# Tile 0 of a conditioned decoder step: routing in one step, taps on VectorE, a seventh unit buffer, and the cached rows' copy in 4 KB pieces

## The chip, the cores and the metric

The kernel runs on one core of a Trainium2 chip. The metric is the time of one execution on the device in microseconds (us); several executions are timed and the median counts. A profiled execution gives, beside its own time, the time of every instruction and of every DMA packet.

## The reference, cut to what matters

One layer of a decoder is applied to 512 prompt rows and to 8 x 4 sample rows, all float32, model width 1024.

```
h   = rms_norm(x) * (1 + scale1) + shift1
z   = h @ w_in                      # q, six k/v column groups, gates, conv input (glu)
o_attn = compressed, selected and windowed attention, gated
u   = glu_a * sigmoid(glu_b);  y[t] = sum_k conv_w[k] * u[t + k] + conv_b    # 31 taps, 512 channels
x  += gate1 * concat(rms_norm(o_attn), silu(layer_norm(y)) * scale) @ w_out
h2  = rms_norm(x) * (1 + scale2) + shift2
q   = (h2 @ q_w).reshape(8 heads, 2, 128);  s = q . sub_keys      # 128 scores for each of 2 halves
s1, i1 = top_k(s[0], 16);  s2, i2 = top_k(s[1], 16)
top_s, pos = top_k(all 256 sums of s1 and s2, 16);  expert = i1 * 128 + i2 at pos
x  += gate2 * sum over 8 heads x 16 experts of softmax(top_s) * gelu(h2 . u[expert]) * v[expert]
new_win_sample = the cached window rows moved up by 4, then 4 new rows; other caches likewise
```

For each of 8 samples `new_win_sample` takes over 508 cached rows of 1 KB each (2 x 2 x 64 floats) unchanged. That is a copy from HBM to HBM of 8 x 520 KB, and no arithmetic depends on it.

## The kernel before, in words

The rows are worked in five tiles, four of 128 prompt rows and one of 32 sample rows. Each of tiles 0 to 3 has 8 x 16 = 128 experts per row, and the sample tile 32 more steps, 544 steps in all. One step gathers from HBM, for every partition, the 8 KB of one expert (u and v), 1 MB for the tile, into one of ten ring rows (`expert_rows`, GpSimd's indirect DMA at L2777). VectorE multiplies u with h2 and sums (L2724), ScalarE makes gelu, weight and a diagonal, and TensorE adds the weighted v into PSUM (L1460).

Everything else of a tile ("side work") is written as stages: `x`, `glu`, `z`, `cmp`, `att`, `conv`, `mix` (the product with w_out, L1189), `query0` and `query1` (the product with q_w, L1205, and the scores, L1292 and L1264), and `topk0` and `topk1` (the routing of four heads each). `make_plan` lays the stages into windows of slots; lanes of one item run side by side, and every engine runs its part of each slot in that one order. Window 0 and the one behind it hold all of tile 0 up to `topk0`; no expert step is consumed before that is through, since there are no experts yet. From then on slots are dealt out between the steps.

**Weights** come in units of 1 MB (128 partitions x 8 KB) into few homes. `weight_units` lists the units in the order of use: `ada` (adaLN), `in`, `w1`, `wo`, `pq` (q_w). `homes_of` gives each the home that was used longest ago: three slots of `weight_units`, and early in the program three more, ring row 4 (`EARLY_ROW`), `h_rows` and `gate_or_shift_and_scale`. SyncE (SP) issues all plain loads and stores from one queue in one order (`sp_program`). For each unit it first does what `aside(key)` says, then waits until TensorE has used the home's unit before, then issues.

**Tile 0 is special.** `topk0` runs in two steps of two heads (`routed`), so that GpSimd can begin gathering after the first. The keys for the scores are loaded into `mod_a` and `mod_b` (L2910, L2913), outside the unit order. Of the 31 taps over four groups of 128 channels, GpSimd does the first two groups (L2754, L2756) and VectorE the other two (L2198, L2201). The cached rows' copy (L2914, 4 MB) is issued before the load of unit `pq` 3, with outermost dimension 8 (one for each sample):

```
if key == ("pq", 0, 3):
    sp.wait_ge(e.s_h2, 1)
    sp.dma_start(e.mod_b, io["keys_unit"][:, D:]).then_inc(e.s_k0[1], 16)
    sp.dma_start(io["new_win_sample"][0, :, 0:WIN - DT].rearrange("b w a g d -> b w (a g d)"),
                 io["cache_win_kv"][0, :, DT:].rearrange("b w a g d -> b w (a g d)")).then_inc(e.s_store, 16)
```

## Time and profile before

| | us |
|---|---|
| median of 3 executions | 2018.53 (2012.03 to 2022.49) |
| the profiled execution | 2007.81, its span 2005.9 |
| TensorE busy | 1472.7 (73%) |
| VectorE busy | 1259.0 (63%) |
| GpSimd busy | 839.2 (42%) |
| ScalarE busy | 760.7 (38%) |
| moved by DMA | 756.73 MB, mean 377 GB/s |

The profile has a page with the busy share of each engine and of the 16 DMA engines in 40 slices of the span. Other views give windows of any length with the DMA engines' mean busy share and rate, the instructions of an engine in order of time with the idle time before each and what ended it, DMA issues with their sizes, and groups of instructions by line.

### The profile page before, as it was taken

Reading aid. Unit: us, or ns where it says so; the run is one execution under the profiler, and the core shown is the slowest. Engines: PE = TensorE matmul, PEld = TensorE weight load, DVE = VectorE, ACT = ScalarE, POOL = GpSimd, SP = SyncE. Lnnn points to the kernel's source line nnn. Section 1 sums busy time; section 2 is a strip of 40 time slices with the busy share of each in tenths; the row PEclk is TensorE's granted clock in tenths of the full one; section 3 lists DMA queues with packets and bytes.
Section 4 is the critical chain, followed back from the end, with each engine's and each line's share of the span. In section 5 each row is a group of like instructions: output and inputs, shape, how many; then the busy total and the mean of one; then the engine's idle time right before and its main releaser. Section 6 shows DMA issues by size and latency. Waiting matters only on the chain.

```text
span 2005.9 us, 27852 instructions
## 1 busy us (share of the span) xinstructions
PE 1472.7 (73%) x9567; PEld 829.9 (41%) x9567; DVE 1259.0 (63%) x3345; ACT 760.7 (38%) x2179; POOL 839.2 (42%) x738
## 2 busy tenths in 40 slices
PE   7775677878679897958667879775979685866532
PEld 4644544445445443535313446443545241423100
DVE  1564585965888689935996645883456554343754
ACT  1431244853265466733236642231222233242322
POOL 0520032433334354523333432772764767432532
PEclk9878788888889898878868989797999878786866
DMA  9778889999999899999999999898999999999996
GB/s 394 253 265 307 330 357 420 402 383 388 420 397 403 345 417 407 396 412 382 419 421 379 420 405 392 319 416 313 353 407 381 394 406 339 399 412 379 371 411 274
DMA packets 132287, 756.73 MB, mean 377 GB/s; under 512 B 17134, under 2 KB 36494, under 8 KB 46050
## 3 DMA queue, kind: packets, MB, share of 16 engines
q0 software_dynamic: 82432, 578.86, 71.6%
q1 hardware_dynamic: 49715, 176.10, 22.8%
q8 instruction: 77, 1.26, 0.3%
q14 instruction: 63, 0.52, 0.1%
HBM read 750.19 MB, written 9.29 MB: 379 GB/s over the span
## 4 chain that ended last, share of the span: by engine, by line
PE 33%; DMA 20%; DVE 16%; issue 7%; POOL 5%; ACT 5%; SPq 0%; POOLq 0%; ACTq 0%; DVEq 0%
PE bank L1460 12%; DMA expert_rows<-in_expert_uv,expert_index 11%; DVE expert_rows L2724 6%; PE bank L1333 4%; PE bank L1205 3%; POOL expert_rows L2777 3%; PE bank L857 3%; PE bank L1189 3%; POOL weight_units L2781 2%; DMA gate_or_shift_and_scale<-mod_dram 2%; PE bank L794 2%; DMA weight_units<-in_w_out_units 1%; DMA weight_units<-in_peer_q_units 1%; DVE gate_or_shift_and_scale L2201 1%; DMA out_y_prompt<-x_rows 1%
## 5 line engine op out<-in xcount | busy, mean ns | idle before, releaser
L2777 POOL DMA_INDIRECT expert_rows<-in_expert_uv,expert_index x544 | 648.5, 1192 | 1027.4 <-PE bank L1460 806.0
L2724 DVE CUSTOM_DVE_ANT_0 expert_rows<-expert_rows,h_rows 128x1024 f32<-128x1024 f32 x544 | 659.7, 1221 | 357.8 <-DMA expert_rows<-in_expert_uv,expert_index 349.5
L1460 PE MATMUL bank<-expert_rows,weight_diagonals 64*64 64x512 f32 x4096 | 589.2, 701 | 127.5 <-ACT weight_diagonals L2042 105.1
L2022 ACT ACTIVATE group_gelu<-group_dots 128x2 f32<-128x2 f32 x272 | 55.1, 203 | 763.8 <-DVE group_dots L2724 759.8
L1460 PEld LDWEIGHTS bank<-expert_rows,weight_diagonals 64*64 64x64 f32 x4096 | 149.4, 150 | 412.4 <-issue 221.7
L2042 ACT ACTIVATE weight_diagonals<-consts_sb,group_weights 128x64 f32<-128x64 f32 (+1 forms) x544 | 158.1, 338 | 17.0 <-ACT group_weights L2032 0.4
L1205 PE MATMUL bank<-stage_room,weight_units 128*128 128x128 f32 x1024 | 130.9, 288 | 34.8 <-DMA weight_units<-in_peer_q_units 33.2
L1205 PEld LDWEIGHTS bank<-stage_room,weight_units 128*128 128x128 f32 x1024 | 124.2, 201 | 58.0 <-DMA weight_units<-in_peer_q_units 37.3
L2032 ACT ACTIVATE group_weights<-group_gelu,expert_gate 128x1 f32<-128x1 f32 x544 | 130.5, 287 | 9.5
L2201 DVE SCALAR_TENSOR_TENSOR conv_out<-stage_room,small_weights,conv_out 128x128 f32<-128x128 f32 (+1 forms) x420 | 125.7, 347 | 0.1
L2022 ACT ACT_TABLE_LOAD x74 | 94.9, 1283 | 1.3
L1189 PE MATMUL bank<-weight_units,stage_room 128*128 128x256 f32 (+1 forms) x304 | 75.1, 406 | 21.7 <-issue 10.3
L1189 PEld LDWEIGHTS bank<-weight_units,stage_room 128*128 128x128 f32 (+1 forms) x304 | 54.6, 184 | 48.4 <-issue 21.6
L1463 PE MATMUL bank<-expert_rows,weight_diagonals 128*32 128x512 f32 x128 | 28.9, 1053 | 55.3 <-ACT weight_diagonals L2042 42.1
L1333 PE MATMUL bank<-weight_units,prompt_bias 128*128 128x256 f32 x256 | 64.7, 403 | 0.0
L1333 PE MATMUL bank<-weight_units,stage_room 128*128 128x256 f32 x256 | 61.7, 393 | 0.0
L857 PE MATMUL bank<-weight_units,stage_room 128*128 128x256 f32 (+1 forms) x240 | 58.5, 396 | 3.1 <-issue 3.1
L2527 DVE MAX8 stage_room<-stage_room 128x8 f32<-128x128 f32 (+1 forms) x102 | 27.5, 325 | 50.1 <-ACT stage_room L1909 25.3
L1333 PEld LDWEIGHTS bank<-weight_units,prompt_bias 128*128 128x128 f32 x256 | 49.0, 199 | 20.0 <-issue 13.8
L1333 PEld LDWEIGHTS bank<-weight_units,stage_room 128*128 128x128 f32 x256 | 48.1, 194 | 16.4 <-issue 10.5
L2476 DVE TENSOR_TENSOR stage_room<-bank,gate_or_shift_and_scale 128x256 f32<-128x256 f32 (+1 forms) x20 | 8.4, 422 | 67.5 <-PE bank L1189 67.5
L857 PEld LDWEIGHTS bank<-weight_units,stage_room 128*128 128x128 f32 (+1 forms) x240 | 39.2, 170 | 25.4 <-issue 14.1
(387 smaller groups left out, 2003.6 us busy)
## 6 DMA issues: line engine op xcount, KB each, us to landing
weight_units<-in_peer_q_units SPq DMA_DIRECT2D x40, 1024.0 KB
weight_units<-in_w_in_units SPq DMA_DIRECT2D x22, 1024.0 KB
weight_units<-in_w_out_units SPq DMA_DIRECT2D x19, 1024.0 KB
weight_units<-in_w_ada_units SPq DMA_DIRECT2D x14, 1024.0 KB
weight_units<-in_w_units SPq DMA_DIRECT2D x11, 1024.0 KB
expert_rows<-in_expert_uv,expert_index POOLq DMA_INDIRECT x544, 12.1
gate_or_shift_and_scale<-mod_dram SPq DMA_DIRECT2D x11, 512.0 KB
expert_rows<-in_w_ada_units SPq DMA_DIRECT2D x5, 1024.0 KB, 6.7
```

Source lines behind the costliest of these rows:

```text
L794: last = mm(out[:, 0:TOKENS], w[:, k, a * P:(a + 1) * P], e.hT[i][:, k * TOKENS:(k + 1) * TOKENS], start=(k == 0), stop=(k == KD - 1))
L857: last = mm(out[0:r, c * 256:(c + 1) * 256], hT(t, k), w[:, k], start=(k == 0), stop=(k == KD - 1))
L1189: last = mm(out[0:r, 0:256], e.catT[:, k, 0:r], w[:, k], start=(k == 0), stop=(k == KD - 1))
L1205: last = mm(out[:, c:c + r], w[:, k, a * P:(a + 1) * P], e.h2T[:, k, 0:r], start=(k == 0), stop=(k == KD - 1))
L1333: last = mm(dst, w1[:, one, s, hh * P:(hh + 1) * P], w[:, :, :, s], start=False, stop=(one == 1 and s == 7))
L1460: last = mm(e.bank[2 * a + c][o * HD:(o + 1) * HD, :], e.diag[ps, m % (NG * GR)], e.ring[ps, m % RING, cs], start=first, stop=final)
L2022: do(e.act_v[:, p], e.dots[:, p], ACT.Gelu_apprx_tanh).then_inc(e.s_gelu, 1)
L2032: do(e.wv[:, p, j:j + 1], e.act_v[:, p, j:j + 1], ACT.Copy, scale=e.gsm[:, i % 2, o + j:o + j + 1]).then_inc(e.s_w, 1)
L2042: do(e.diag[:, p * GR + j, 0:unit.shape[1]], unit, ACT.Copy, scale=e.wv[:, p, j:j + 1]).then_inc(e.s_d, 1)
L2201: ins = vec.scalar_tensor_tensor(out, src, w[:, ct, k:k + 1], out, ALU.mult, ALU.add)
L2724: vec.tensor_tensor_reduce(out=row, in0=row, in1=e.h2[:, i % 2], scale=1.0, scalar=0.0, op0=ALU.mult, op1=ALU.add, accum_out=e.dots[:, q % ...
L2777: pool.indirect_dma_start(e.ring[:, n % RING], None, e.io["expert_uv"], bass.IndirectOffsetOnAxis(ap=e.eidx[:, i % 2, j:j + 1], axis=0)).t ...
```

## The change

Five edits, all in the part of tile 0 ahead of the first expert step.

1. `topk0` of tile 0 is one step of four heads, as in the other tiles. The plan runs `query0`, then `query1` beside `topk0`. TensorE computes all four `pq` units of a half before its scores.
2. The keys come as units of the common order (`keys`, 0, half) into the three slots, and no more into `mod_a` and `mod_b`.
3. VectorE does all 124 taps, by pairs of channel groups, beginning when two groups of conv input are there. GpSimd does none.
4. Ring row 5, which GpSimd's taps used, becomes one more home for early units (seven in all).
5. The cached rows' copy is issued at unit `wo` 0, ahead of the four `wo` loads, in pieces of four rows (4 KB), with the piece's number (127) as outermost dimension and the sample (8) inside it. Loading gate2's rows moves from `pq` 7 to `in` 6 of tile 1.

```diff
-EARLY_HOMES = 6
-EARLY_ROW = 4
+EARLY_ROWS = (4, 5)
+EARLY_HOMES = SLOTS + len(EARLY_ROWS) + 2
...
-        "query0": lambda i: [("pq", i, u) for u in range(4)] + ([("keys", i, 0)] if 0 < i < PT else []),
+        "query0": lambda i: [("pq", i, u) for u in range(4)] + ([("keys", i, 0)] if i < PT else []),
...
-        homes = list(range(SLOTS)) + [3] * (j < row_until) + [4] * (j < h2_until) + [5] * (j < mods_until)
+        homes = list(range(SLOTS)) + [3, 4] * (j < row_until) + [5] * (j < h2_until) + [6] * (j < mods_until)
...
+    def conv_first(slots, w):
+        n = 0
+        for pair in ((0, 1), (2, 3)):
+            e.early.freed(dve, ("glu", 0, pair[1], 0))
+            for k in range(CK):
+                for ct in pair:
+                    out, src = e.convo[:, ct], e.cu[:, ct, k:k + P]
+                    if k == 0:
+                        ins = vec.tensor_scalar(out, src, w[:, ct, 0:1], w[:, ct, CK:CK + 1], ALU.mult, ALU.add)
+                    else:
+                        dve.wait_ge(e.s_tap, n - 1)
+                        ins = vec.scalar_tensor_tensor(out, src, w[:, ct, k:k + 1], out, ALU.mult, ALU.add)
+                    ins.then_inc(e.s_tap, 1)
...
-        if key == ("pq", 0, 2):
-            sp.wait_ge(e.s_x1, 1)
-            sp.dma_start(e.mod_a, io["keys_unit"][:, 0:D]).then_inc(e.s_k0[0], 16)
-        if key == ("pq", 0, 3):
-            sp.wait_ge(e.s_h2, 1)
-            sp.dma_start(e.mod_b, io["keys_unit"][:, D:]).then_inc(e.s_k0[1], 16)
-            sp.dma_start(io["new_win_sample"][0, :, 0:WIN - DT].rearrange("b w a g d -> b w (a g d)"),
-                         io["cache_win_kv"][0, :, DT:].rearrange("b w a g d -> b w (a g d)")).then_inc(e.s_store, 16)
+        if key == ("wo", 0, 0):
+            sp.dma_start(io["new_win_sample"][0, :, 0:WIN - DT].rearrange("b (u w) a g d -> u b (w a g d)", w=DT),
+                         io["cache_win_kv"][0, :, DT:].rearrange("b (u w) a g d -> u b (w a g d)", w=DT)
+                         ).then_inc(e.s_store, 16)
             sp.dma_start(io["new_conv_sample"][0, :, 0:CK - 1 - DT, :], io["state_conv"][0, :, DT:, :]
                          ).then_inc(e.s_store, 16)
```

**SP's order.** Before, the copy stands behind the `wo`, `ada` and first `pq` loads. The last number of a row is the shape that the instruction carries.

```order
L2800 DMA weight_units<-in_w_ada_units 128x2048 x3
L2808 DMA weight_units<-in_peer_q_units 128x2048 x2
L2910 DMA gate_or_shift_and_scale<-in_keys_unit 128x1024
L2808 DMA weight_units<-in_peer_q_units 128x2048
L2913 DMA gate_or_shift_and_scale<-in_keys_unit 128x1024
L2914 DMA out_new_win_sample<-in_cache_win_kv 8x8x16256
L2916 DMA out_new_conv_sample<-in_state_conv 8x13312
L2808 DMA weight_units<-in_peer_q_units 128x2048 x4
```

Now it stands behind the last `ada` unit of the second group (u = 19), and all four `wo` loads, the rows of shift and scale, the last `ada` loads and all `pq` loads are behind it.

```order
L2745 DMA h_rows<-in_w_ada_units 128x2048
L2854 DMA out_new_win_sample<-in_cache_win_kv 127x8x1024
L2857 DMA out_new_conv_sample<-in_state_conv 8x13312
L2774 DMA gate_or_shift_and_scale<-mod_dram 128x1024
L2751 DMA weight_units<-in_w_out_units 128x2048 x3
L2784 DMA mod_dram<-expert_rows 9x1024
L2751 DMA expert_rows<-in_w_out_units 128x2048
L2784 DMA mod_dram<-expert_rows 9x1024
L2774 DMA expert_rows<-mod_dram 128x1024
L2774 DMA gate_or_shift_and_scale<-mod_dram 128x1024
L2745 DMA expert_rows<-in_w_ada_units 128x2048
```

The copy moved past the fourteen loads between, and its outermost count went from 8 to 127.

**TensorE from h2 to the first expert step.** L1205 and L1199 are the product with q_w (16 matmuls a unit, which the trace shows as 32), L1292, L1264 and L1255 the scores. Before:

```order
L1276 MATMUL bank<-consts_sb,h_rows 128x128 x8
L1205 MATMUL bank<-stage_room,weight_units 128x128 x32
L1292 MATMUL bank<-gate_or_shift_and_scale,stage_room 128x128 x4
L1205 MATMUL bank<-stage_room,weight_units 128x128 x32
L1292 MATMUL bank<-gate_or_shift_and_scale,stage_room 128x128 x4
L1205 MATMUL bank<-stage_room,weight_units 128x128 x64
L1264 MATMUL bank<-gate_or_shift_and_scale,stage_room 128x128 x8
```

Now:

```order
L1267 MATMUL bank<-consts_sb,h_rows 128x128 x8
L1199 MATMUL bank<-stage_room,weight_units 128x128 x64
L1255 MATMUL bank<-weight_units,stage_room 128x128 x8
L1199 MATMUL bank<-stage_room,weight_units 128x128 x64
L1255 MATMUL bank<-weight_units,stage_room 128x128 x8
```

The first scores moved from behind two units to behind four, and the keys are read from the unit slots.

## Rows read from the trace of the kernel before

**Rows 1.** The page: DMA share in tenths and rate, in 40 slices of the span.

```profile
DMA  9778889999999899999999999898999999999996
GB/s 394 253 265 307 330 357 420 402 383 388 420 397 403 345 417 407 396 412 382 419 421 379 420 405 392 319 416 313 353 407 381 394 406 339 399 412 379 371 411 274
```

**Rows 2.** Windows: length, busy us of PE, PEld, DVE, ACT, POOL, clock, DMA share, GB/s.

```profile
186.00:192.00 6.00, 0.00 (x0) 0.00 (x0) 5.69 (x17) 0.23 (x1) 0.00 (x0) 0.50 0.43 184
190.00:194.00 4.00, 0.00 (x0) 0.00 (x0) 3.73 (x10) 0.00 (x0) 0.00 (x0) 0.50 0.52 223
...
200.00:205.00 5.00, 5.00 (x26) 5.00 (x25) 0.00 (x0) 0.00 (x0) 3.78 (x5) 0.50 1.01 421
240.00:245.00 5.00, 1.38 (x7) 1.39 (x8) 3.56 (x16) 2.78 (x5) 0.00 (x0) 0.76 0.33 139
245.00:250.00 5.00, 2.86 (x13) 2.46 (x12) 4.90 (x21) 4.85 (x13) 0.00 (x0) 0.50 0.00 0
```

**Rows 3.** TensorE in order of time: start, length, what, idle before and its releaser.

```profile
141.34 6.50 PE L1189 MATMUL bank<-h_rows,stage_room 128*128 128x256 f32 x16 [4.24 <-DVE stage_room L2468]
...
168.01 7.41 PE L1205 MATMUL bank<-stage_room,weight_units 128*128 128x128 f32 x64 [0.73 <-ACT stage_room L1861]
176.14 1.13 PE L1292 MATMUL bank<-gate_or_shift_and_scale,stage_room 128*128 128x128 f32 x8 [0.72 <-issue]
177.11 3.74 PE L1205 MATMUL bank<-stage_room,weight_units 128*128 128x128 f32 x32
199.01 6.69 PE L1205 MATMUL bank<-stage_room,weight_units 128*128 128x128 f32 x32 [18.16 <-DMA weight_units<-in_peer_q_units]
...
229.98 6.57 PE L1205 MATMUL bank<-stage_room,weight_units 128*128 128x128 f32 x32 [10.95 <-DMA weight_units<-in_peer_q_units]
```

**Rows 4.** SP's queue in order of time.

```profile
122.70 0.33 SPq L2800 DMA_DIRECT2D expert_rows<-in_w_ada_units  x1
...
166.19 0.88 SPq L2914 DMA_DIRECT2D out_new_win_sample<-in_cache_win_kv  x1
...
171.88 34.18 SPq L2808 DMA_DIRECT2D weight_units<-in_peer_q_units  x4
```

**Rows 5.** DMA issues of 0 to 300 us: count, KB each, median us to landing.

```profile
out_new_win_sample<-in_cache_win_kv SPq DMA_DIRECT2D x1, 4064.0 KB
...
small_weights<-in_small SPq DMA_DIRECT2D x1, 487.0 KB, 4.3
out_new_conv_sample<-in_state_conv SPq DMA_DIRECT2D x1, 416.0 KB
expert_rows<-in_expert_uv,expert_index POOLq DMA_INDIRECT x24, 14.3
```

**Rows 6.** VectorE's taps: five beside GpSimd's taps, what stands behind them, five alone.

```profile
89.77 3.75 DVE L2201 SCALAR_TENSOR_TENSOR conv_out<-stage_room,small_weights,conv_out 128x128 f32<-128x128 f32 x5
...
94.95 0.15 DVE L2302 TENSOR_TENSOR hidden_bias<-bank,small_weights 128x4 f32<-128x4 f32 x1
...
121.83 1.38 DVE L2201 SCALAR_TENSOR_TENSOR conv_out<-stage_room,small_weights,conv_out 128x128 f32<-128x128 f32 x5
```

**Rows 7.** VectorE: a routing step of two heads, a grid operation of four, step 0's dot.

```profile
177.92 0.87 DVE L2527 MAX8 stage_room<-stage_room 128x8 f32<-128x128 f32 x4 [11.22 <-ACT stage_room L1909]
...
188.79 0.69 DVE L2564 TENSOR_TENSOR stage_room<-stage_room,consts_sb 128x512 f32<-128x512 f32 x1
...
193.37 0.18 DVE L2572 CAST expert_index<-stage_room 128x32 int32<-128x32 f32 x1
...
239.97 1.23 DVE L2724 CUSTOM_DVE_ANT_0 expert_rows<-expert_rows,h_rows 128x1024 f32<-128x1024 f32 x1
...
282.33 1.23 DVE L2564 TENSOR_TENSOR stage_room<-stage_room,consts_sb 128x1024 f32<-128x1024 f32 x1
```

**Rows 8.** GpSimd: the first gather and the eleventh.

```profile
194.49 1.11 POOL L2777 DMA_INDIRECT expert_rows<-in_expert_uv,expert_index  x1 [77.88 <-DVE expert_index L2572]
...
...
257.05 1.90 POOL L2777 DMA_INDIRECT expert_rows<-in_expert_uv,expert_index  x1 [50.26 <-PE bank L1460]
```

More of the change, by code:

```diff
@@ L341, in memory @@
     x_odd = e.sb("odd_x_rows", [P, D])
-    e.homes = [e.unit[:, j] for j in range(SLOTS)] + [e.ring[:, EARLY_ROW], e.h2[:].rearrange("p a n -> p (a n)"), team]
+    e.homes = [e.unit[:, j] for j in range(SLOTS)]
+    e.homes += [e.ring[:, a] for a in EARLY_ROWS] + [e.h2[:].rearrange("p a n -> p (a n)"), team]
     e.xr = [(x_even, x_odd)[i % 2] for i in range(TILES)]
@@ L1282, in query0 @@
             yield from sample_queries(0)
-            return
-        if i == 0:
-            for q in range(2):
-                yield from queries(i, range(2 * q, 2 * q + 2))
-                if q == 0:
-                    keys = key_half(i, 0)
-                prod.freed(pe, ("pq", i, q))
-                out = prod.open(pe, ("scores", i, q))
-                for a in range(4):
-                    last = mm(out[:, a * P:(a + 1) * P], e.q2T[:, 4 * q + a, 0:P], keys[:, 4 * q + a], start=True, stop=True)
-                last.then_inc(prod.ready, 1)
-                yield
             return
@@ L1899, in query_half @@
             return
-        if i == 0 and half == 0:
-            for q in range(2):
-                for _ in range(8):
-                    yield
-                out = prod.wait(act, ("pq", i, q))
-                nc.scalar.copy(e.q2T[:, 4 * q:4 * q + 4].rearrange("p a n -> p (a n)"), out[:]
-                               ).then_inc(prod.free(("pq", i, q)), 1)
-                yield
-                out = prod.wait(act, ("scores", i, q))
-                nc.scalar.copy(e.scores[0][:, 4 * q:4 * q + 4].rearrange("p a n -> p (a n)"), out[:]
-                               ).then_inc(prod.free(("scores", i, q)), 1)
-            return
         for q in range(2 * half, 2 * half + 2):
@@ L1927, in topk @@
     def topk(i, part):
-        if i == 0 and part == 0:
-            for a in range(2):
-                for _ in range(7 if a == 0 else 10):
-                    yield
-                act.wait_ge(e.s_sx if a else e.s_sx0, 1)
-                g = e.gsm[:, 0, 2 * a * TK:2 * (a + 1) * TK]
-                do(g, g, ACT.Exp).then_inc(e.s_gx if a else e.s_gx0, 1)
-            return
         n = 4 if i < PT else 2
@@ L2178, in conv @@
         if i == 0:
-            e.early.freed(dve, ("glu", i, 3, 0))
-        elif i < LATE:
+            yield from conv_first(slots, w)
+            return
+        if i < LATE:
             prod.freed(dve, ("glu", i, 3))
@@ L2188, in conv @@
             link(vec.tensor_copy(e.cs[:, :, :, CK - 1:], e.us[:].rearrange("p c (b t) -> p c b t", b=NB)))
-        cts = range(2, 4) if i == 0 else range(4)
-        total = len(cts) * CK
-        for n in range(total):
-            k, ct = n // len(cts), cts[n % len(cts)]
+        for n in range(4 * CK):
+            k, ct = n // 4, n % 4
             if i < PT:
@@ L2745, in pool_program @@
 def pool_program(e, pool):
-    each = e.nc.gpsimd
-    link = Chain(pool, e.s_pch)
-    w = e.col("conv").rearrange("p (c k) -> p c k", c=4)[:, 0:2]
-    cu, convo = e.cu[:, 0:2], e.convo[:, 0:2]
-    part = e.ring[:, 5, 0:2 * P].rearrange("p (c n) -> p c n", c=2)
-    e.early.freed(pool, ("glu", 0, 1, 0))
-    for k in range(CK):
-        link(each.tensor_tensor(part if k else convo, cu[:, :, k:k + P], span(w[:, :, k], 2, P), ALU.mult))
-        add = part if k else span(w[:, :, CK], 2, P)
-        ins = each.tensor_tensor(convo, convo, add, ALU.add)
-        if k + 1 < CK:
-            link(ins)
-    ins.then_inc(e.s_pc, 1)
-    pool.wait_ge(e.s_pc, 1)
     for m in range(3):
         pool.wait_ge(e.s_md[m], 16)
-    pool.wait_ge(*e.given[max(j for j, home in enumerate(e.home) if home == SLOTS)])
+    for a in range(SLOTS, SLOTS + len(EARLY_ROWS)):
+        pool.wait_ge(*e.given[max(j for j, home in enumerate(e.home) if home == a)])
     due = pool_pages(e)
```

86 lines of the change are left out of this document (30 added, 56 removed).

## The prediction

> **What bounds the kernel now.** I read the slices first, to see what is scarce over the whole span. The DMA engines are busy for nine tenths or more of most slices, and the best rate, about 421 GB/s, appears in many of them [rows 1]. The second view is the windows, for the stretches where that is not so. All of them lie in tile 0, ahead of and just behind the first expert step: 0.43 to 0.52 of the DMA engines while the cached rows are copied, nothing at all from 245 to 250 us [rows 2]. The third view is TensorE in order of time. From 141.3 us, the first `wo` product, the path runs through TensorE: `wo`, the last `ada`, h2, the queries, scores, routing, first dot at 239.97 [rows 3, 7]. It holds two large waits for weights, 18.16 us for unit `pq` 3 and 10.95 us for `pq` 7 [rows 3]. Behind the first dot the plan deals out the same slots to the same steps in both kernels, so what the change does to the total is by how much it moves that first dot, and what DMA work is still owed then.
>
> **The copy (edit 5) is the term that decides.** Before, it is issued at 166.19, and `pq` 3, first of four loads issued from 171.88 on, is used only at 199.01 [rows 3, 4]. Near its end, with next to nothing beside it, the DMA share is 0.52 and 0.43 at 223 and 184 GB/s [rows 2]. That is 7 to 8 of 16 engines, each at its full pace: 421 / 16 = 26.3 GB/s in the full window, 223 / 8 = 27.9 here. The instruction carries 8x8x16256, outermost count 8. So the copy is cut along its outermost dimension, one share for each of 8 engines, and 4064 KB [rows 5], 4.16 MB, take 0.52 MB / 26.3 GB/s = 20 us on each. A load issued behind it must pass through all 16 engines, waits in the same queues, and is as late as its share on the busiest.
>
> Now the outermost count is 127, with 8 inside. If shares must be equal, 127 (a prime) can be dealt to one engine or to 127, and there are 16: the whole copy goes through one. It then takes 4.16 MB / 26.3 GB/s = 158 us. Bounds: 149 us at 27.9 GB/s for an engine, 181 us at 184 / 8 = 23. The pieces shrink from 65 KB to 4 KB; no row has a piece of 4 KB from HBM to HBM, and units of 8 KB rows move at the full 421 GB/s [rows 2], so I add nothing for it and let the 181 us stand for it. I take equal shares: the rows show a hard cut by the outermost count, which left half of the engines without work although each sample's 520 KB was itself in eight rows of 65 KB. They cannot exclude shares of 8, 8, ... 7, since 8 is dealt out evenly either way; that is the first rival.
>
> The Trainium skill, page "DMA: Bandwidth & Descriptors", section "Queues, rings and completion order" with the one on why a DMA adds 16 to its semaphore, states just this rule: for a DMA from SP the slowest dimension picks the largest number of engines up to 16 that divides it, and 127 gives 1. The trace agrees for a count of 8; no row here shows a count that 16 engines cannot share evenly.
>
> When is it issued? Before, the last `ada` load of that group (u = 19) leaves at 122.70 [rows 4]; it waited for TensorE to use the unit that held its home. With seven homes it waits for a unit one earlier, and the compress branch ahead of it moves up too (next part). I take 112 us, between 107 and 122.7, and add 2.5 us for that 1 MB unit (1.05 MB / 421 GB/s) which is ahead in the queues. The copy ends at 112 + 2.5 + 158 = 272.5. On the same engine stand behind it the conv history (416 KB on 8 engines [rows 5], 52 KB each, 2.0 us), gate1's rows (512 KB on 16, 1.2 us) and `wo` 0 (2.5 us), and about 1 us until TensorE sees it: 279.2. TensorE began `wo` 0 at 141.34 [rows 3]. **The stall is 137.9 us**; bounds 107 + 149 + 8 = 264 gives +123, 122.7 + 2.5 + 181 + 7 = 313 gives +172.
>
> What else is queued: SP waits, ahead of the rows of shift2, for a 36 KB store of `mod_dram` that also sits behind the copy, so the last four `ada` loads leave only then. They need 10 us of DMA, and TensorE spends more than that on the four `wo` units (6.50 us on the first alone [rows 3]), so I add 1 us. From `wo` 0 to the first query product nothing else changes: 168.01 - 141.34 = 26.7 us.
>
> **Taps on VectorE (edit 3).** Beside GpSimd's taps five cost 3.75 us, alone 1.38 [rows 6], 0.28 each. Before, about half of VectorE's 62 taps ran at the slow pace and half at the fast, 31 x 0.75 + 31 x 0.28 = 32 us; now 124 x 0.28 = 34 us, begun some 12 us earlier. What stands behind them moves up: `hidden_bias` at 94.95 [rows 6] now comes behind 49 fast taps, 13.6 us, with the attention's own operations between them, near 92. Down the chain (compressed keys, their attention) I get 4 us at `wo` 0, bounds 0 and 7. In this branch it is worth nothing in itself, since `wo` 0 waits for the copy 140 us longer; it only brings the copy's issue forward. Were that cover gone, it would count in full. The seventh home (edit 4) likewise: one 1 MB load earlier, no wait of its own removed.
>
> **Queries, keys and routing (edits 1 and 2).** From the first query product on, in us behind it. Before: four units and the wait up to the second scores, then the first dot at 239.97 - 168.01 = 72.0 [rows 3, 7]. Now: four `pq` units back to back, 7.41 + 2 x 3.74 = 14.9. Can the loads follow? A unit needs 2.5 us of DMA and about 2 us to land (487 KB landed in 4.3 us [rows 5]); three slots give it 7 us, so yes. Scores and their copy to VectorE: in the rows 175.42 to 177.92, 2.5. Routing four heads: two heads took 177.92 to 193.55, 15.6; twice that is 31.2, less 7 x (2 x 0.69 - 1.23 = 0.15) = 1.0 for the grid operations done once [rows 7], less 1.4 for a dozen small ones: 28.8. GpSimd starts 0.9 later (193.55 to 194.49 [rows 8]), and the first 1 MB lands behind 5.5 us, bounds 4.3 and 14.3 [rows 5]. Sum 14.9 + 2.5 + 28.8 + 0.9 + 5.5 = 52.6, against 72.0: **a gain of 19.4 us**, bounds 11 and 21. The second half (`query1`) ends near 35 and is off the path.
>
> What was gathered early was worth nothing: ten gathers from 194.49 fill the ring, the eleventh waits until 257.05 [rows 8], and meanwhile they took 10 MB x 1 / 421 GB/s = 25 us of DMA in front of `pq` 7, hence its 10.95 us. But they are owed now. At the first dot the new kernel is about 10 MB behind, some 25 us; before, the DMA engines idled there: 0.33 and 0.00 of them from 240 to 250 [rows 2], and the ring was full until 257.05 [rows 8], in all some 15 us. Steps follow each other there at about 3.6 us and use 1 MB each, so gathers keep ahead; units of tile 1 come late by what is left. I charge 3 us, less 1.4 us since x of tile 1 is normed before the dot and not behind it: +1.6, bounds 0 and 9.
>
> **Sum.** 137.9 + 1 - 19.4 + 1.6 = **+121 us**. Against the profiled execution: 2007.8 + 121 = 2129. That execution was 10.7 us under the median of the three, and medians are compared, so I forecast 2018.5 + 121 = **2139 us**. Lowest: 123 - 21 - 6 (spread of the three) = +96, 2114; I take 2110. Highest: 172 + 1 - 11 + 9 = +171, 2189; I take 2187.
>
> **Rivals.**
>
> *A, the copy is spread.* If 127 is dealt as 8, 8, ... 7, or along the dimension of 8, it takes 10 to 20 us from 112 on, when the DMA engines were idle or half idle, and the `wo` loads land 5 us or more before 141. For it: the rows bear uneven shares as well, and each other edit removes a wait that is plain in the trace. Against: the eight engines follow the outermost count. Then edits 3 and 4 count: -4 - 19.4 + 1.6 = -22: 1997 us, faster. 0.15.
>
> *B, spread, but the debt eats the gain.* The ten gathers and tile 1's units meet in one burst: first landing 14.3 in place of 5.5, debt 9 in place of 3, no gain from the taps: -19.4 + 8.8 + 7.6 = -3: 2016 us, no change. For it: the slices behind 260 us are at 400 GB/s and more [rows 1], so there is little room to catch up. It decides if the first landing takes over 10 us. 0.03.
>
> *C, one engine, and its small pieces are dear.* If a 4 KB piece costs more than its bytes, say 0.25 us in place of 0.156, 1016 pieces take 254 us and the time is 2235. Against: both sides of the transfer are plain rows. 0.02.
>
> **How the numbers follow.** One engine at the priced rate 0.80, A 0.15, B 0.03, C 0.02; the copy is either on one engine or spread, and the half-empty windows of rows 2 speak for a strict deal by the outermost count. The likeliest gives 2139. Its range 2110 to 2187 holds nearly all of its 0.80, so it is given alone. A measurement of this kernel can tell about 0.5%, 10 us, from no change: faster 0.15, same 0.03, slower 0.82.
>
> **What would show it.** In the profile of the changed kernel: a stretch of 120 us or more before the first `wo` product with TensorE idle and a DMA share near 1/16, about 26 GB/s; its wait put down to the `wo` load. Then `pq` units with no wait on DMA, one routing of four heads some 29 us long, the first gather about 47 us behind the first query product, the first dot near 53. Taps at 0.28 us with `hidden_bias` near 92 us. From the first dot on the same lengths as before. The forecast is wrong if the DMA share stays at a half or more behind the copy's issue and the `wo` products start near 137: then it is rival A.

## The result, and the profile after

| | before | after |
|---|---|---|
| median of 4 executions, us | 2015.28 | 2135.14 |
| the profiled execution, and its span | 2007.81, 2005.9 | 2132.21, 2130.4 |
| mean rate of DMA over the span, GB/s | 377 | 355 |

The ratio is 1.0592, with a 95% interval of 1.0527 to 1.0657: the changed kernel is 120 us slower. One of its four executions, 2178.09 us at a mean granted clock of 0.735 where the others have 0.81 to 0.82, is left out of the ratio. The forecast was 2139 with a range of 2110 to 2187.

The page of the changed kernel answers to [rows 1]. The third to fifth of its 40 slices of 53 us hold the loss:

```profile
DMA  9720077999999998999999999989899999999996
GB/s 399 254 97 26 36 280 286 420 421 404 347 377 417 385 418 344 418 396 397 414 419 421 383 420 408 396 332 412 312 372 402 388 396 378 355 408 374 401 413 279
```

In windows (columns as in [rows 2]) the copy shows as one sixteenth of the DMA engines at 26 to 27 GB/s, for as long as it runs. From 262.5 us on the loads behind it are issued and pass on the other engines, up to the full rate, while the copy still runs on its own. A second lull at 275 to 285 us is that one engine's share of these loads:

```profile
120.00:140.00 20.00, 7.87 (x67) 5.27 (x66) 10.74 (x34) 8.64 (x20) 0.00 (x0) 0.72 0.07 27
140.00:160.00 20.00, 0.00 (x0) 0.00 (x0) 0.00 (x0) 0.00 (x0) 0.00 (x0) 0.50 0.06 26
...
270.00:275.00 5.00, 0.00 (x0) 0.00 (x0) 0.00 (x0) 0.00 (x0) 0.00 (x0) 0.50 1.01 427
275.00:280.00 5.00, 0.00 (x0) 0.00 (x0) 0.00 (x0) 0.00 (x0) 0.00 (x0) 0.50 0.53 223
280.00:285.00 5.00, 2.85 (x7) 2.35 (x8) 0.00 (x0) 0.00 (x0) 0.00 (x0) 0.50 0.06 26
```

SP's queue, which answers to [rows 4]. L2854 issues the copy. L2857, the conv history behind it, is 149.64 us in the issuing itself: SP can hand over no further DMA until most of the copy has gone.

```profile
111.43 0.49 SPq L2745 DMA_DIRECT2D h_rows<-in_w_ada_units  x1
111.96 0.84 SPq L2854 DMA_DIRECT2D out_new_win_sample<-in_cache_win_kv  x1
112.86 149.64 SPq L2857 DMA_DIRECT2D out_new_conv_sample<-in_state_conv  x1
262.61 0.63 SPq L2774 DMA_DIRECT2D gate_or_shift_and_scale<-mod_dram  x1
263.29 4.14 SPq L2751 DMA_DIRECT2D weight_units<-in_w_out_units  x3
```

TensorE, which answers to [rows 3]. L1183 is the product with w_out, at 282.15 in place of 141.34, and L1199 is the product with q_w, in which no unit waits for its load any more:

```profile
132.93 1.97 PE L1174 MATMUL bank<-consts_sb,stage_room 128*128 128x128 f32 x8 [6.30 <-DVE stage_room L2436]
282.15 12.37 PE L1183 MATMUL bank<-weight_units,stage_room 128*128 128x256 f32 x48 [147.25 <-issue]
...
308.32 14.56 PE L1199 MATMUL bank<-stage_room,weight_units 128*128 128x128 f32 x128 [0.72 <-ACT stage_room L1840]
323.60 2.02 PE L1255 MATMUL bank<-weight_units,stage_room 128*128 128x128 f32 x16 [0.72 <-issue]
```

The wait of 147.25 us is put down to "issue", so to nothing that the profile shows, and not to the `wo` load. That the load ended it is read from the queue and the packets: its issue begins at 263.29; seven of the conv history's eight pieces run from 263.3 on, and the eighth, which shares the copy's engine, only from 276.03 to 278.00; the next loads, `wo` 0 among them, come behind it in the same queue.

VectorE, which answers to [rows 6] and [rows 7] (taps, hidden_bias, routing of four heads from its first MAX8 to its indices, first dot), and GpSimd, which answers to [rows 8] (first and eleventh gather):

```profile
78.99 3.76 DVE L2140 SCALAR_TENSOR_TENSOR conv_out<-stage_room,small_weights,conv_out 128x128 f32<-128x128 f32 x14
...
95.74 0.15 DVE L2275 TENSOR_TENSOR hidden_bias<-bank,small_weights 128x4 f32<-128x4 f32 x1
```

```profile
325.39 0.88 DVE L2490 MAX8 stage_room<-stage_room 128x8 f32<-128x128 f32 x4 [18.36 <-ACT stage_room L1890]
...
354.14 0.20 DVE L2535 CAST expert_index<-stage_room 128x64 int32<-128x64 f32 x1
...
361.19 1.23 DVE L2687 CUSTOM_DVE_ANT_0 expert_rows<-expert_rows,h_rows 128x1024 f32<-128x1024 f32 x1 [5.47 <-DMA expert_rows<-in_expert_uv,expert_index]
```

```profile
355.27 1.07 POOL L2722 DMA_INDIRECT expert_rows<-in_expert_uv,expert_index  x1 [354.81 <-DVE expert_index L2535]
...
376.08 0.94 POOL L2722 DMA_INDIRECT expert_rows<-in_expert_uv,expert_index  x1 [7.39 <-PE bank L1439]
```

The first dot is at 361.19 in place of 239.97, 121.2 us later; the span is 124.5 us longer. All but 3.3 us of the loss is there before the first expert step.

### The profile page after: what moved, and what is told of

Its sections match the earlier page's. It is cut to its first block, busy times and chain, and to the rows that moved or that the text cites. A ratio compares the mean times of both kernels' runs of the same rounds, so it can differ in the third digit from the quotient of the medians.

```text
span 2130.4 us, 27830 instructions
## 1 busy us (share of the span) xinstructions
PE 1476.8 (69%) x9567; PEld 830.8 (39%) x9567; DVE 1257.3 (59%) x3390; ACT 760.4 (36%) x2178; POOL 787.3 (37%) x676
## 3 DMA queue, kind: packets, MB, share of 16 engines
q1 hardware_dynamic: 50660, 176.10, 21.5%
## 4 chain that ended last, share of the span: by engine, by line
PE 33%; DMA 15%; DVE 15%; issue 7%; ACT 6%; POOL 6%; SPq 0%; POOLq 0%; ACTq 0%; DVEq 0%
PE bank L1439 12%; DMA expert_rows<-in_expert_uv,expert_index 10%; DVE expert_rows L2687 5%; PE bank L1312 4%; POOL weight_units L2726 3%; POOL expert_rows L2722 3%; PE bank L1183 3%; PE bank L1199 3%; PE bank L853 2%; DMA weight_units<-in_peer_q_units 2%; PE bank L790 2%; PE bank L1119 1%; DMA gate_or_shift_and_scale<-mod_dram 1%; DVE gate_or_shift_and_scale L2174 1%; ACT stage_room L1772 1%
## 5 line engine op out<-in xcount | busy, mean ns | idle before, releaser
L1439 PE MATMUL bank<-expert_rows,weight_diagonals 64*64 64x512 f32 x4096 | 592.0, 704 | 132.1 <-ACT weight_diagonals L1997 109.7
L1183 PE MATMUL bank<-weight_units,stage_room 128*128 128x256 f32 (+1 forms) x304 | 79.0, 422 | 159.7 <-issue 150.6
L1183 PEld LDWEIGHTS bank<-weight_units,stage_room 128*128 128x128 f32 (+1 forms) x304 | 57.8, 195 | 186.5 <-issue 161.3
L1199 PEld LDWEIGHTS bank<-stage_room,weight_units 128*128 128x128 f32 x1024 | 118.8, 194 | 28.3 <-issue 19.5
L1199 PE MATMUL bank<-stage_room,weight_units 128*128 128x128 f32 x1024 | 124.8, 281 | 4.9 <-DMA weight_units<-in_peer_q_units 3.3
L2174 DVE SCALAR_TENSOR_TENSOR conv_out<-stage_room,small_weights,conv_out 128x128 f32<-128x128 f32 (+1 forms) x360 | 95.6, 312 | 0.0
L1119 PE MATMUL bank<-prompt_keys_values,queries_turned 64*128 64x256 f32 (+2 forms) x96 | 48.5, 606 | 2.8 <-ACT stage_room L1787 2.8
```

The source lines that it names most:

```text
L1119: last = mm(out[:, c:c + m], q, k[lo:lo + HD, 0:m], start=True, stop=True)
L1183: last = mm(out[0:r, 0:256], e.catT[:, k, 0:r], w[:, k], start=(k == 0), stop=(k == KD - 1))
L1199: last = mm(out[:, c:c + r], w[:, k, a * P:(a + 1) * P], e.h2T[:, k, 0:r], start=(k == 0), stop=(k == KD - 1))
L1439: last = mm(e.bank[2 * a + c][o * HD:(o + 1) * HD, :], e.diag[ps, m % (NG * GR)], e.ring[ps, m % RING, cs], start=first, stop=final)
L2174: ins = vec.scalar_tensor_tensor(out, src, w[:, ct, k:k + 1], out, ALU.mult, ALU.add)
```

## Experiments

Ratios are to the kernel before, measured on the same chip as each group of runs: 2022.3 us for the first four, 2024.8 for the next four (GpSimd's taps, six homes, two steps, 254), 2012.4 for the last four. Times of different groups compare by these ratios. "First query product" is the first product with q_w, "first dot" the dot of step 0.

### 1. What makes the copy slow: count, piece or place

Four kernels, each the changed one with nothing but the copy's form altered; both access patterns are rearranged alike.

**Outermost count 8 again**, at the new place:

```diff
-  ...rearrange("b (u w) a g d -> u b (w a g d)", w=DT)
+  ...rearrange("b w a g d -> b w (a g d)")
```

> The changed kernel with one thing put back: the cached rows' copy has the outermost count 8 again (8x8x16256 in place of 127x8x1024), at its new place ahead of `wo` 0. Theory (the outermost count sets how many DMA engines share the copy): it ends some 20 us behind its issue at 112, `wo` 0 begins near 139 in place of 282, so 143 us come back: 2135 - 143 = 1992 us, 1985 to 2003. Rival (the new place costs: any copy of 4 MB ahead of `wo` 0 holds it up): 20 to 40 us of the stall stay, 2012 to 2032.

Measured: 2001.35 us, ratio 0.9896 (0.9862 to 0.9931). 134 us less than the changed kernel, so nearly all of the 143 came back. `wo` 0 begins at 144.38 and not at 139, and it waited 9.16 us:

```profile
144.38 13.23 PE L1183 MATMUL bank<-weight_units,stage_room 128*128 128x256 f32 x48 [9.16 <-issue]
```

Its window from 135 to 140 us has half of the engines free, as [rows 2] had:

```profile
135.00:140.00 5.00, 0.22 (x2) 0.00 (x0) 0.69 (x1) 3.34 (x8) 0.00 (x0) 0.50 0.33 140
```

So most of the stall was the count. What is left of the wait is the copy's on 8 engines at this place: 5.2 us, 9.16 against the 3.92 of the next kernel.

**Outermost counts 112 and 15**, pieces of 4 KB kept:

```diff
+            for first, last, w in ((0, 448, 4), (448, 508, 4)):
+                sp.dma_start(io["new_win_sample"][0, :, first:last].rearrange("b (u w) a g d -> u b (w a g d)", w=w),
+                             io["cache_win_kv"][0, :, DT + first:DT + last].rearrange("b (u w) a g d -> u b (w a g d)", w=w)
+                             ).then_inc(e.s_store, 16)
```

> The changed kernel with its 4 KB pieces, at its new place, in two DMAs of outermost counts 112 and 15 in place of one of 127 (448 and 60 rows of each sample). Theory (outermost count): 112 is shared by 16 engines and 15 by 15, all pieces at 0.155 us make 1016 x 0.155 / 16 = 10 us, `wo` 0 near 139, 1992 us, 1985 to 2003. Rival (4 KB pieces from HBM to HBM are what is slow, or pile up in SP's queue): the stretch of TensorE idle stays over 50 us and the time over 2040.

Measured: 2000.76 us, ratio 0.9908 (0.9869 to 0.9947). `wo` 0 and the first dot:

```profile
137.63 12.44 PE L1183 MATMUL bank<-weight_units,stage_room 128*128 128x256 f32 x48 [3.92 <-DVE stage_room L2441]
```

```profile
217.79 1.22 DVE L2687 CUSTOM_DVE_ANT_0 expert_rows<-expert_rows,h_rows 128x1024 f32<-128x1024 f32 x1 [5.41 <-DMA expert_rows<-in_expert_uv,expert_index]
```

The same 1016 pieces of 4 KB at the same place, and the stall is gone: `wo` 0 waits for VectorE and no more for a load. Neither the size of the pieces nor the place was the cause.

**Outermost count 126**, one piece a sample less in the large DMA (the edit is the loop above over `((0, 504, 4), (504, 508, 1))`):

> The changed kernel with one 4 KB piece a sample taken out of the large DMA: outermost count 126 (504 rows of each sample) and a second DMA of the last 4 rows with outermost count 4. Theory (the engines are the largest number up to 16 that divides the outermost count): 126 goes to 14 engines, 1008 pieces x 0.155 / 14 = 11 us, 1992 us, 1985 to 2003. Rival (any count over 16 that isn't a multiple of 16 goes to one engine, or to few): one engine, 2135 us; 126 mod 16 = 14 alone tells nothing apart from it, one busy engine in 14 would.

Measured: 1998.48 us, ratio 0.987 (0.9801 to 0.9938).

```profile
138.01 12.37 PE L1183 MATMUL bank<-weight_units,stage_room 128*128 128x256 f32 x48 [3.92 <-DVE stage_room L2441]
```

126 is fast and 127 is not. That falls in with the rule that the engines must divide the outermost count (126 = 14 x 9), and refutes one engine for every count that isn't a multiple of 16. The trace's DMA packets show the number itself: from 121 to 128 us mostly 14 pieces of 4 KB are under way at a time, in the kernel with 112 and 15 mostly 16.

**Outermost count 254**, pieces of 2 rows (`w=2`):

> The changed kernel with the copy cut in pieces of 2 rows, 2 KB, outermost count 254 in place of 127 (254x8x512). Theory (largest number up to 16 that divides the count): 254 gives 2 engines, 2032 pieces in all, 1016 on each; if a 2 KB piece takes half of 0.155 us the copy lasts 79 us and the rate is 53 GB/s, `wo` 0 begins near 205 and the time is near 2058; if a 2 KB piece takes as long as one of 4 KB, it lasts 158 us at 26 GB/s, 2135 us. Rival (any count that 16 doesn't divide goes to one engine): one engine, 158 us at least, 2135 us or more, at 26 GB/s too; the number of pieces under way at a time tells these apart.

Measured: 2058.73 us, one execution; forecast 2058. The rate while it runs, `wo` 0, and SP's issue of the next DMA:

```profile
140.00:160.00 20.00, 0.00 (x0) 0.00 (x0) 0.00 (x0) 0.00 (x0) 0.00 (x0) 0.50 0.13 51
```

```profile
204.83 12.77 PE L1183 MATMUL bank<-weight_units,stage_room 128*128 128x256 f32 x48 [71.46 <-issue]
```

```profile
111.56 78.09 SPq L2858 DMA_DIRECT2D out_new_conv_sample<-in_state_conv  x1
```

Share 0.13, two sixteenths: two engines, the largest number up to 16 that divides 254 = 2 x 127. The trace has 125 packets of 2 KB in 5 us, so 0.080 us each on an engine, against 32 of 4 KB in 5 us, 0.155 us each, with 127: bytes, not pieces, set the time. Four counts, 8, 126, 254 and 127, with 8, 14, 2 and 1 pieces under way at a time, are told apart as the largest number up to 16 that divides the count says.

### 2. The same form at the old place

```diff
 if key == ("pq", 0, 3):
-    ...rearrange("b w a g d -> b w (a g d)")
+    ...rearrange("b (u w) a g d -> u b (w a g d)", w=DT)
```

> The kernel before with one thing changed: the cached rows' copy, at its old place behind `pq` 3, as 127x8x1024. Theory (one engine for 158 us): issued at 166 the copy ends near 327, SP and the loads of `pq` 3 and on are held, `pq` 3 begins near 331 in place of 199, +132 us, less up to 11 us for the wait ahead of `pq` 7 that has gone by then: 2136 to 2150 us. Rival (the harm of the change lies in its new place): under 2060.

Measured: 2173.04 us, ratio 1.073 (1.0654 to 1.0805). The form alone costs more here than in the changed kernel, and more than I expected. Unit `pq` 3, and two windows of the copy:

```profile
366.54 5.60 PE L1205 MATMUL bank<-stage_room,weight_units 128*128 128x128 f32 x32 [180.87 <-DMA weight_units<-in_peer_q_units]
```

```profile
200.00:250.00 50.00, 0.00 (x0) 0.00 (x0) 0.00 (x0) 0.00 (x0) 8.85 (x10) 0.50 0.55 223
250.00:300.00 50.00, 0.00 (x0) 0.00 (x0) 0.00 (x0) 0.00 (x0) 0.00 (x0) 0.50 0.06 26
```

From 200 to 250 GpSimd's ten gathers get through while SP's loads do not, and the copy pays: 23 of its pieces pass in 10 us from 210 to 240, against 64 or 65 alone, counted in the trace's DMA packets. Some 35 us at that pace put off (6.4 - 2.3) x 35 = 143 pieces, 143 x 0.155 = 22 us. I had left that out. Of the 35.5 us by which `pq` 3 is later than I gave, this is most; the copy's later issue (170.82, I took 166) is 5 more, and the rest isn't told apart. The ten gathers used the engine by another queue than SP's; that is the next experiment.

### 3. The same copy through another queue

The 127x8x1024 copy is issued by ScalarE, behind its copy of tile 0's compressed keys.

```diff
         nc.scalar.copy(e.kcT[:, 0:hi], out[:, 0:hi]).then_inc(prod.free(("kcT", i)), 1)
+        if i == 0:
+            nc.scalar.dma_start(...same two access patterns...).then_inc(e.s_store, 16)
```

> The changed kernel with the 127x8x1024 copy issued from ScalarE's DMA queue (behind its copy of the compressed keys of tile 0, near 108 us) and not from SP's; all else as changed. Theory (the copy is on one engine, and the loads are held because they stand behind it in the same queue; an engine takes two queues in turn, as the gathers passed the copy in the run of before with 127): a unit's share on that engine takes 8 x (0.309 + 0.155) = 3.7 us in place of 2.5, `wo` 0 begins at 138 to 142, the copy lasts up to 158 x 64/23 = 440 us, and while it does DMA runs at two thirds of its rate: the first dot at 218 to 230, the total 2010 to 2060. Rival (the engine itself is shut while the copy is on it, whichever queue it came by): `wo` 0 near 282, 2135 us.

Measured: 2096.52 us, one execution. The front is as the theory says, `wo` 0 at 137.30, so the engine isn't shut. The tail is dearer than I gave it: the time is 36 us above the top of my range, 2060. The same windows, first of this kernel, then of the one with 112 and 15:

```profile
137.30 12.50 PE L1183 MATMUL bank<-weight_units,stage_room 128*128 128x256 f32 x48 [3.92 <-DVE stage_room L2446]
```

```profile
260.00:360.00 100.00, 57.16 (x326) 29.27 (x326) 52.71 (x131) 31.65 (x81) 19.68 (x19) 0.78 0.79 306
400.00:500.00 100.00, 64.21 (x325) 32.17 (x325) 60.43 (x196) 45.57 (x132) 21.74 (x20) 0.69 0.64 238
```

```profile
260.00:360.00 100.00, 78.33 (x486) 41.29 (x487) 75.14 (x207) 51.12 (x145) 35.39 (x30) 0.79 1.01 421
400.00:500.00 100.00, 81.13 (x580) 54.65 (x580) 57.60 (x159) 35.01 (x102) 33.04 (x29) 0.91 0.98 394
```

The copy's packets run from 109.7 to 590 us, 480 in place of 158. As long as they do, the whole core gets 306 and 238 GB/s in place of 421 and 394. My reading is that every 1 MB load or gather is as late as its share on that one engine; the trace does not name the engine of a packet, so this is argued. That the copy is the cause is seen from when the loss arises: the first dot is at 228.99, 11.2 us behind the kernel with 112 and 15, the hundredth step, at 585 us, is 120 us behind, and from there to the end, with the copy gone, the distance grows no more (105 to 117 us). So two things stalled the changed kernel: one engine for the whole copy, and the order of SP's queue, which made all of it come before the `wo` loads. Another queue takes the second away and spreads the first over 480 us.

### 4. What the other edits are worth

Here the copy is in the 112 and 15 form, so that it hides nothing, in all kernels but the first. That one is the kernel before once more, for its trace:

> The kernel before once more, for its trace on the same chip. Theory (the trace of before that the rows come from was of an execution in which TensorE's products of the first `in` unit ran at the full granted clock, while every later trace has them at half until 43 us): here they are at half too, `wo` 0 begins near 146 in place of 141.3, the first dot near 245 in place of 240, and the time is nearer 2022 than 2008. Rival (the slow stretch comes with the changed kernel's order): `wo` 0 at 141.3.

Measured: 2008.91 us, one execution. TensorE's first `in` unit, `wo` 0, unit `pq` 3, and VectorE's first dot:

```profile
38.55 5.87 PE L948 MATMUL bank<-weight_units,expert_rows 128*128 128x256 f32 x16 [2.02 <-ACT expert_rows L1547]
...
146.58 6.46 PE L1189 MATMUL bank<-h_rows,stage_room 128*128 128x256 f32 x16 [4.16 <-DVE stage_room L2468]
...
204.39 6.58 PE L1205 MATMUL bank<-stage_room,weight_units 128*128 128x128 f32 x32 [18.36 <-DMA weight_units<-in_peer_q_units]
```

```profile
245.60 1.22 DVE L2724 CUSTOM_DVE_ANT_0 expert_rows<-expert_rows,h_rows 128x1024 f32<-128x1024 f32 x1
```

Half of the theory held: the products of the first `in` unit are slow here too, `wo` 0 is at 146.58 and the first dot at 245.60. The other half did not: the time is 2008.91, no nearer to 2022. The trace that the rows ahead of the prediction come from is the odd one, with

```profile
36.17 3.72 PE L948 MATMUL bank<-weight_units,expert_rows 128*128 128x256 f32 x16 [2.02 <-ACT expert_rows L1547]
```

In all thirteen other traces, of the changed kernel and of every experiment, the first products are 0.427 us apart until 41 to 43 us and 0.216 then. That is the granted clock. In nine of these traces the windows show it, as in this one of the kernel before with its copy spread (the last experiment below): 0.50, which is 1.2 GHz, up to 43.1 us, then 1.00, which is 2.4 GHz.

```profile
38.00:41.00 3.00, 3.00 (x8) 2.37 (x9) 0.00 (x0) 0.00 (x0) 0.00 (x0) 0.50 0.98 415
44.00:47.00 3.00, 3.00 (x16) 2.64 (x15) 0.00 (x0) 0.00 (x0) 0.00 (x0) 1.00 1.01 418
```

In the other four, among them the trace of the changed kernel and this second one of before, the trace holds no record of the clock before 42.6 to 43.4 us, and a window without a record reads 1.00, whatever the clock was; from the first record on the pace is the fast one. In the odd trace that first record is at 30.95 us. So its clock rose some 11 us earlier, and why it did stays open. What follows for the comparison: differences at the first dot are better taken against 245.6 than against 240.

**GpSimd's taps and six homes again** (edits 3 and 4 undone, the code of before in `conv`, `pool_program` and `homes_of`):

> The kernel of the 112 and 15 copy, with edits 3 and 4 undone: GpSimd's half of the taps and six homes, as before; routing in one step and keys as units stay. Theory (the taps bring 4 us at `wo` 0, the routing 19 to 20 at the first dot): `wo` 0 begins at 141 in place of 137.6, the first dot at 221.5 in place of 217.8, total 2005 against 2001. Rival (the taps bring all the gain, the routing is hidden): first dot near 236.

Measured: 2011.22 us, ratio 0.9924 (0.9891 to 0.9958). SP's copy, `wo` 0, first dot:

```profile
125.77 1.77 SPq L2853 DMA_DIRECT2D out_new_win_sample<-in_cache_win_kv  x2
```

```profile
151.66 5.33 PE L1185 MATMUL bank<-h_rows,stage_room 128*128 128x256 f32 x16 [11.09 <-issue]
```

```profile
231.44 1.23 DVE L2671 CUSTOM_DVE_ANT_0 expert_rows<-expert_rows,h_rows 128x1024 f32<-128x1024 f32 x1 [5.54 <-DMA expert_rows<-in_expert_uv,expert_index]
```

Both were wrong: with routing in one step the taps are worth 13.6 us at the first dot, not 4. They let SP issue the copy at 110.7 in place of 125.8, and only so does it end ahead of the `wo` loads' due time. With it in front at 125.8, `wo` 0 waits 11.09 us.

**Six homes alone**, taps on VectorE:

```diff
-EARLY_ROWS = (4, 5)
+EARLY_ROWS = (4,)
```

> The kernel of the 112 and 15 copy, with the seventh home (edit 4) undone, all else kept. Theory (the seventh home removes no wait of its own): `wo` 0 within 1.5 us of 137.6, first dot within 1.5 us of 217.8, total 2001. Rival (it is what sets the earlier loads of tile 0 free): `wo` 0 3 us or more later. The slow TensorE stretch of the traces with seven homes (products of the first `in` unit at half the granted clock up to 43 us) belongs to the loads' order if it goes away here, to the run if it stays.

Measured: 1997.7 us, ratio 0.9875 (0.9824 to 0.9925), `wo` 0 at 137.04, first dot at 217.93, 0.1 us from 217.79. The seventh home is worth nothing here. The slow first products stay, so they do not come with seven homes.

**Routing in two steps** (edits 1 and 2 undone; taps, homes and the copy at `wo` 0 kept):

> The kernel before, with edits 3 and 4 (all taps on VectorE, seven homes) and the cached rows' copy in two DMAs of 112 and 15 ahead of `wo` 0; queries, keys and routing in two steps stay as before. Theory (the 18.16 us wait for `pq` 3 was the copy's and the keys', the 10.95 us wait for `pq` 7 the first ten gathers'): the first of the two waits shrinks to under 5 us since no copy is queued there, the second stays, and the first dot comes near 240 - 4 - 14 = 222, total near 2005. Then the gain of 19 us that was put down to the routing belongs mostly to the copy's place. Rival (routing in one step itself brings it): first dot at 232 or later, total near 2012.

Measured: 1998.49 us, ratio 0.9892 (0.9836 to 0.9948).

```profile
215.27 1.23 DVE L2740 CUSTOM_DVE_ANT_0 expert_rows<-expert_rows,h_rows 128x1024 f32<-128x1024 f32 x1
```

The first dot is 2.5 us earlier than with one step, and from the first query product (166.19) on it takes 49.1 us, against 52.8. Both waits for `pq` units are gone, the one that I expected to stay too. What is left are some 5 us of small gaps between the products of the last `pq` units, from 200 to 207 us, put down to "issue". Routing in one step brings nothing once the copy is out of the way.

**The kernel before with the copy alone moved ahead of `wo` 0**:

> The kernel before with the copy and the conv history alone moved ahead of `wo` 0, in the 112 and 15 form; taps on GpSimd and VectorE, six homes, two steps of routing, as before. Theory (what the run with two steps and the run with GpSimd's taps told apart adds up): the copy is issued near 126, `wo` 0 begins near 151 as in the run with GpSimd's taps, no wait for `pq` 3 or `pq` 7 is left, the first dot is 77 us behind `wo` 0, near 228; total near 2012 against 2022 of before. Rival (without the earlier taps the move gives nothing): first dot at 238 or later.

Measured: 1996.97 us, ratio 0.9923 (0.9895 to 0.9952). `wo` 0, `pq` 7, first dot:

```profile
150.94 5.61 PE L1189 MATMUL bank<-h_rows,stage_room 128*128 128x256 f32 x16 [10.85 <-issue]
...
214.28 3.84 PE L1205 MATMUL bank<-stage_room,weight_units 128*128 128x128 f32 x32 [2.14 <-DMA weight_units<-in_peer_q_units]
```

```profile
221.53 1.23 DVE L2724 CUSTOM_DVE_ANT_0 expert_rows<-expert_rows,h_rows 128x1024 f32<-128x1024 f32 x1
```

`wo` 0 is where I had it. The first dot is 6.5 us earlier than I gave, and 6.3 us behind the run with two steps and VectorE's taps: with routing in two steps, the taps are worth 6.3 us at the first dot and not 13.6.

**The kernel before with the copy at its old place, spread**:

> The kernel before with one thing changed: the cached rows' copy at its old place, behind `pq` 3, in two DMAs of 112x8x1024 and 15x8x1024 in place of 8x8x16256. Theory: it takes 10 us of 16 engines and not 20 us of 8, so the wait for `pq` 3 shrinks from 18 to 8 us and the first dot comes 8 to 10 us earlier, unless the ten gathers of the first two heads, which still stand ahead of `pq` 7, take it back: 2008 to 2017 on this chip. Rival (the wait for `pq` 3 is set by something else): no change of the first dot.

Measured: 2005.02 us, ratio 0.9959 (0.9935 to 0.9982), first dot at 235.44, 10.2 us earlier. The wait for `pq` 3 halved as expected, that for `pq` 7 stayed:

```profile
194.33 6.59 PE L1205 MATMUL bank<-stage_room,weight_units 128*128 128x128 f32 x32 [9.06 <-DMA weight_units<-in_peer_q_units]
...
225.78 6.25 PE L1205 MATMUL bank<-stage_room,weight_units 128*128 128x128 f32 x32 [10.65 <-DMA weight_units<-in_peer_q_units]
```

Together, in us, with the length behind the first dot as span less first dot. Each row is one profiled execution, and executions of one kernel differ by 29 us (the kernel before, 2007 to 2036 on one chip), so the last column is rough:

| copy | taps | routing | `wo` 0 | first query product to first dot | first dot | behind it |
|---|---|---|---|---|---|---|
| 8 engines, old place (before again) | GpSimd | two | 146.6 | 72.4 | 245.6 | 1761.2 |
| spread, old place | GpSimd | two | 145.0 | 63.0 | 235.4 | 1758.5 |
| spread, at `wo` 0 | GpSimd | two | 150.9 | 44.4 | 221.5 | 1768.9 |
| spread, at `wo` 0 | GpSimd | one | 151.7 | 52.9 | 231.4 | 1778.0 |
| spread, at `wo` 0 | VectorE | two | 138.7 | 49.1 | 215.3 | 1772.7 |
| spread, at `wo` 0 | VectorE | one | 137.6 | 52.8 | 217.8 | 1771.5 |
| one engine, at `wo` 0 (after) | VectorE | one | 282.2 | 52.9 | 361.2 | 1769.2 |

## Why the prediction was right, and where not

**The copy on one engine: right, in mechanism and size.** Issue at 111.96 (I took 112), a rate of 26 to 27 GB/s (26.3), `wo` 0 at 282.15 (279.2), the stall 140.8 us against the rows' 141.34 (137.9), and 135.6 against the second trace of before, 146.58, whose clock rose as late. Inside the sum two small terms were off. The copy's packets begin at 118.0 and not 114.5, since two 1 MB units were still ahead in the queue and not one; 158 us on, it ends at 276 (272.5). Behind it I had 6.7 us for the conv history, gate1's rows and `wo` 0; they took 6.1. I had these loads waiting in the queues; that SP itself would be held for 149.64 us was not foreseen, and seems to have cost nothing here, since it came free 13 us before the copy's engine did. The rule of the Trainium skill, page "DMA: Bandwidth & Descriptors", section on why a DMA adds 16 to its semaphore, that a DMA takes the largest number of engines up to 16 that divides its slowest dimension, held for every count tried, 8, 126, 127 and 254.

**What stands behind: right.** From `wo` 0 to the first query product 26.2 us against 26.7 and 1 for the late `ada` loads; they cost at most 0.41 us of waiting each.

**Queries to first dot: the size right, the cause wrong.** 52.9 us, forecast 52.6, against 72.0: 19.1 us gained. Its parts: units 14.6 (14.9), scores 2.5 (2.5), routing 28.9, from 325.39 to the end of the indices at 354.34 (28.8), GpSimd 0.9 (0.9), landing 5.9 (5.5); the first gather 46.95 us behind the first query product (47). `query1` ended at 342.7, 34.3 us behind it (35). But I booked the gain on edits 1 and 2, queries and routing in one step. The failed step is the one that set four `pq` units back to back against two large waits, as if the order of the plan had removed them. The size came out all the same, since the terms of the new stretch were right and no wait was left in it, for another reason than mine. The runs show that the copy's leaving was enough: with it at `wo` 0 and two steps of routing the same stretch takes 44.4 and 49.1 us, 8.5 and 3.7 us less than with one step. No run has routing in one step with the copy at its old place, so whether edits 1 and 2 alone could have removed the waits too stays open. The first two heads' gathers do not delay `pq` 7 by themselves, as I had it from [rows 3] and [rows 8]: where the copy is gone that wait is 2.14 us or none, and only where the copy is still ahead of `pq` 3 is it 10.65.

**Taps: mis-sized.** 0.27 us each (0.28), right. `hidden_bias` at 95.74, forecast 92; against 99.49 in the trace of before with the same slow start it is 3.7 us earlier, forecast 3. At `wo` 0, read from the kernels where no copy holds it, 137.5 against 145.0 to 146.6: about 8 us, and I had 4 with 7 as the bound. In the changed kernel it is hidden, as predicted. With the copy spread at `wo` 0 it is 13.6 us at the first dot with routing in one step, since SP's issue of the copy comes forward with it, and 6.3 with two. In the time it can't be told from noise: 0.9908 with, 0.9924 without, and the intervals overlap.

**The seventh home: right,** nothing of its own.

**The debt: probably too small.** Against the trace of the rows the span grew 3.3 us more than the first dot, against the second trace of before 8.0; forecast 1.6, bounds 0 and 9. The kernels with the copy at the old place, on 8 engines or spread, need 1758 to 1766 us behind the first dot (1785 with it on one engine), those with it at `wo` 0 1769 to 1781 over all runs (the copy in ScalarE's queue apart). The medians, which are less rough, say 1 to 9 us: the changed kernel with 112 and 15 has its first dot 27.8 us earlier and its median 21.5 us lower, the kernel before with the copy alone moved 24.1 and 15.4, that with GpSimd's taps 14.2 and 13.6. So part of an earlier first dot seems to be given back, more than I charged. Ten owed gathers don't explain it alone, since the two-step kernels, which gather early, pay it too. What does was not tried.

**The sum.** Stall, `wo` 0 to the first query product, queries to first dot, debt: forecast 137.9 + 1 - 19.4 + 1.6 = 121. Measured against the second trace of before: 135.6 - 0.4 - 19.5 + 8.0 = 123.6. By medians the loss is 120. The stall carries it.

**Signs.** The lull, the share and the rate came as promised. The wait was put down to "issue" and not to the `wo` load: that sign was wrong, though the cause was right.

**Rival A,** the copy spread, was put at 1997 with 0.15. It did not occur, but the kernel that it describes exists: the changed one with 112 and 15 took 2000.76 where before took 2022.3, 21.5 us less; A said 22. That is in part luck: it booked 19.4 on the routing, 4 on the taps and 1.6 on the debt.

A version better than both is among the runs. The changed kernel with the copy spread, with six homes or with routing in two steps, takes 1998 us, 0.9875 and 0.9892 of before. Moving the spread copy alone in the kernel before, two edits of a few lines, gives 1996.97, 0.9923 (0.9895 to 0.9952). These intervals overlap: no run shows that edits 1 to 4 add to it.

## What to carry to other kernels

Read the shape that a DMA instruction carries: in all counts tried here the number of engines that share it was the largest up to 16 that divides its outermost count, and 127, a prime, put 4 MB on one of 16 engines, with everything behind it in the same queue held. A transfer that nothing waits for still costs what stands behind it, so choose its place by what follows in the queue, and try the place alone before rebuilding the stage around it: here a gain that seemed to come with a new plan came with the copy's leaving. Take the trace of the kernel before more than once when differences of 5 us at a mark are read, and compare when the granted clock rose in each.

## What was unexpected in the hardware

- SP was 149.64 us in issuing one DMA behind the copy (78.09 with two engines, 176.63 at the old place). It came free when some 85 of the copy's 1016 pieces were left (262.5 to 276 us at 0.155 each), so a small transfer behind a long one on one engine blocks the issuing engine too, and with it loads for other engines.
- One engine shared with another queue gave the copy 23 or 24 pieces of 4 KB in 10 us beside the gathers, and 21 in the mean beside all of the core's loads and gathers, in place of 64. In the second case the whole core's rate fell to 306 and 238 GB/s from 421 and 394.
- A piece of 4 KB from HBM to HBM took 0.155 us on an engine and one of 2 KB 0.080: at these sizes pieces cost their bytes.
- TensorE's first `in` products ran 0.427 us apart at a granted 0.50 and 0.216 at 1.00. The clock rose between 41.8 and 43.9 us in all traces but one, where it rose at 30.95, and that moved `wo` 0 and the first dot by 5 us. A window for which the trace holds no record of the clock reads 1.00 even so.
